# The shifted bias written and read back in four pieces, and the memory's attention begun beside q's last unit

## The reference, cut to what matters

```
z = h @ w_in                                    # mixer; one of its parts is dilated attention, which
bias = rel_bias_table[bucket].transpose(2,0,1)  # adds a bias for each head and each distance q - k
q = (h @ wq).reshape(b, s, 4, 128)              # memory cross attention: 4 heads of 128
scores = einsum('bshd,bmhd->bhsm', q, k) * 128 ** -0.5
o = einsum('bhsm,bmhd->bshd', softmax(scores), v).reshape(b, s, 512)
return o @ wo
```

## Time and profile before

| | |
|---|---|
| median of 3 runs | 2355.29 us (2349.98 to 2355.97) |
| the profiled execution, its time and its span | 2355.84 us, 2354.1 us |
| TensorE busy | 2253.3 us, 96% of the span |
| VectorE, ScalarE, GpSimd busy | 1362.3, 1067.9, 62.9 us |
| share of TensorE in the chain that ended last | 65% |

### The profile page before, as it was taken

How to read it: one execution, slowest core, us unless ns; L and a number is a source line. 1 busy time by engine, 2 the same in 40 slices (tenths; PEclk the granted TensorE clock), 3 DMA queues, 4 the chain that set the end, 5 groups by cost and what they waited for, 6 DMA issues and landing times.

```text
span 2354.1 us, 31707 instructions
## 1 busy us (share of the span) xinstructions
PE 2253.3 (96%) x12978; PEld 1959.9 (83%) x12978; DVE 1362.3 (58%) x1718; ACT 1067.9 (45%) x1376; POOL 62.9 (3%) x66
## 2 busy tenths in 40 slices
PE   8799999888989999999999999999999999999998
PEld 7788898787877888888888888888986889889776
DVE  5446666566556666767666444655445555544554
ACT  5343542424455544544555334545435443544443
POOL 0000101002000000000000000000000000000000
PEclk9899999899989999999999999999999999999999
DMA  7756440014634555555565555553550556445143
GB/s 279 189 191 202 163 158 1 1 32 154 203 118 134 190 185 188 186 187 187 186 206 191 190 192 196 185 195 120 181 178 19 180 178 222 159 152 174 59 129 140
DMA packets 237804, 375.59 MB, mean 160 GB/s; under 512 B 8535, under 2 KB 110072, under 8 KB 236920
## 3 DMA queue, kind: packets, MB, share of 16 engines
q1 hardware_dynamic: 229596, 362.83, 46.3%
q10 hardware_dynamic: 8092, 11.11, 1.9%
HBM read 369.45 MB, written 4.46 MB: 159 GB/s over the span
## 4 chain that ended last, share of the span: by engine, by line
PE 65%; issue 5%; DVE 4%; ACT 2%; POOL 0%; DVEq 0%; POOLq 0%; ACTq 0%
PE PS L482 16%; PE PS L441 12%; PE PS L443 12%; PE PS L442 12%; PE PS L485 8%; DVE w_lo L359 1%; PE PS L2062 1%; ACT w_hi L354 1%; PE PS L2152 1%; PE PS L2136 1%; PE PS L2046 1%; PE PS L2827 1%; DVE h_both L938 0%; PE PS L921 0%; ACT spare L2074 0%
## 5 line engine op out<-in xcount | busy, mean ns | idle before, releaser
L359 DVE TENSOR_TENSOR w_lo<-raw,w_hi 128x2048 fp32r<-128x2048 f32 (+2 forms) x340 | 766.8, 2256 | 765.2 <-ACT w_hi L354 765.0
L354 ACT ACTIVATE w_hi<-raw 128x2048 fp32r<-128x2048 f32 (+2 forms) x340 | 641.2, 1886 | 876.0 <-PE PS L443 494.4
L482 PE MATMUL PS<-h_both,w_hi 128*128 128x512 f32 x1968 | 541.6, 397 | 12.2 <-DVE w_lo L359 9.4
L441 PE MATMUL PS<-w_hi,h_both 128*128 128x512 f32 (+2 forms) x1344 | 514.9, 383 | 11.7 <-DVE h_both L943 4.5
L442 PE MATMUL PS<-w_lo,h_both 128*128 128x512 f32 (+2 forms) x1344 | 507.2, 377 | 0.0
L443 PE MATMUL PS<-w_hi,h_both 128*128 128x512 f32 (+2 forms) x1088 | 408.3, 375 | 0.0
L482 PEld LDWEIGHTS PS<-h_both,w_hi 128*128 128x128 f32 x1968 | 338.1, 190 | 59.4 <-ACT arena L609 9.6
L485 PEld LDWEIGHTS PS<-h_both,w_lo 128*128 128x128 f32 x1968 | 303.2, 189 | 42.2
L485 PE MATMUL PS<-h_both,w_lo 128*128 128x256 f32 x1968 | 314.0, 281 | 0.0
L441 PEld LDWEIGHTS PS<-w_hi,h_both 128*128 128x128 f32 x1344 | 254.3, 189 | 60.0 <-issue 6.0
L442 PEld LDWEIGHTS PS<-w_lo,h_both 128*128 128x128 f32 x1344 | 254.6, 189 | 45.4
(11 more groups left out here) (569 smaller groups left out, 2003.4 us busy)
## 6 DMA issues: line engine op xcount, KB each, us to landing
raw<-in_w_in SPq DMA_DIRECT2D x132, 1024.0 KB, 5.0
raw<-in_ffn_w_up SPq DMA_DIRECT2D x176, 512.0 KB, 4.3
raw<-in_w_out SPq DMA_DIRECT2D x48, 1024.0 KB, 5.1
raw<-in_ffn_w_down SPq DMA_DIRECT2D x44, 1024.0 KB, 5.0
raw<-in_mem_wkv SPq DMA_DIRECT2D x8, 1024.0 KB, 11.5
raw<-in_mem_wq SPq DMA_DIRECT2D x4, 1024.0 KB, 5.1
raw<-in_mem_wo SPq DMA_DIRECT2D x4, 1024.0 KB, 7.2
raw<-in_w_in SPq DMA_DIRECT2D x4, 768.0 KB, 4.6
```

The costliest lines, as they stand in the source:

```text
L354: act.activation(w_hi[:, slot % 2, :st.n], raw[:, slot, :st.n], ACT.Copy).then_inc(hi_made, 1)
L359: dve.tensor_tensor(w_lo[:, slot % 2, :st.n], raw[:, slot, :st.n], w_hi[:, slot % 2, :st.n].bitcast(F32), ALU.subtract).then_inc(lo_made, 1)
L441: pe.matmul(ps, l_hi, r_hi, start=start, stop=False, skip_group_check=skip)
L482: pe.matmul(sums, wh[:, k, cs], h_both[:, :, kk, :], start=kk == 0, stop=False, skip_group_check=True)
```

## The change

**The bias** is written in four pieces of three heads, each by a DMA of its own, and read back in four pieces. ScalarE issues the writes in stage C, after it has rounded C0, C2, C4 and C6; after C10 it waits for all four writes, issues the first read, and issues the others after C11, C12 and C13. The waits for `rel_back` ask for 64.

**The memory.** Units 2 and 3 of MEM_Q are laid by heads: each holds the rows 1024 to 2047, unit 2 for the columns of heads 0 and 1, unit 3 for those of heads 2 and 3. The attention of heads 0 and 1 begins in the middle of unit 3, that of heads 2 and 3 behind it. Stage MEM_O begins with the blocks of heads 0 and 1 for g0, then turns the rest, then takes the first half of g1, then the second halves of g0 and g1.

```diff
-        ST_MEM_Q = Stage(count, "mem_q", w_cols(I["mem_wq"][0], 0), 1, ch=(0, 512))
+        def mem_q_unit(g, j):
+            return mem_q_rows[:, 4 * j:4 * j + 4, :] if j < 2 else mem_q_rows[:, 8:16, (j - 2) * S:(j - 1) * S]
+        ST_MEM_Q = Stage(count, "mem_q", mem_q_unit, 1, ch=(0, 512))
...
+        def multiply_heads(pe, q, j, ready=None):
+            bank, slot = 2 * q.parity + j - 2, (q.first + j) % 2
...
+            for n, (c, k) in enumerate(order):
+                if n == 8:
+                    if ready:
+                        ready()
+                    yield
...
+        def beside_mem_tensor(pe):
+            yield from multiply_heads(pe, Group(ST_MEM_Q, 0), 3)
+            yield from rounds(4)
+            lanes_made(pe, mem_lanes[:2])
+            turn_pair_tensor(pe, t_o, 0, blocks_of(o_mem))
+            yield
+            pe.wait_ge(t_o.dve, t_o["lo0"])
+            multiply_blocks(pe, Group(ST_MEM_O, 0), 0)
+            lanes_made(pe, mem_lanes[2:])
+            turn_pair_tensor(pe, t_o, 1, blocks_of(o_mem))
+            multiply_blocks(pe, Group(ST_MEM_O, 1), 0)
+            pe.wait_ge(t_o.dve, t_o["lo1"])
+            for g in range(2):
+                multiply_blocks(pe, Group(ST_MEM_O, g), 2)
+            for g in range(2, 4):
+                multiply(pe, Group(ST_MEM_O, g), 0)
+            yield
...
+        def bias_scalar(act):
+            for n in range(4):
+                hs = slice(3 * n, 3 * n + 3)
+                act.dma_start(shifted[hs], arena[hs, WROW:WROW + 384].unsqueeze(1).to_broadcast([3, P, 384]))\
+                   .then_inc(rel_out, 16)
+                yield
+                yield
+            yield
+            yield
+            act.wait_ge(rel_out, 64)
+            for n in range(4):
+                act.dma_start(rel_bias[:, 3 * n:3 * n + 3, :],
+                              bass.AP(shifted.tensor, 3 * n * 384 * P + P - 1, [[383, P], [384 * P, 3], [1, S]]))\
+                   .then_inc(rel_back, 16)
+                yield
...
-            act.dma_start(shifted, arena[0:A_H, WROW:WROW + 384].unsqueeze(1).to_broadcast([A_H, P, 384])).then_inc(rel_out, 16)
...
-            act.wait_ge(rel_out, 16)
-            act.dma_start(rel_bias, bass.AP(shifted.tensor, P - 1, [[383, P], [384 * P, A_H], [1, S]])).then_inc(rel_back, 16)
-            run(products_scalar(act, ST_C, before=end_of(ST_BC), more=True))
+            weave(products_scalar(act, ST_C, before=end_of(ST_BC), more=True), bias_scalar(act))
```

More of the change, by code:

```diff
@@ L335, in load_units @@
                     sp.wait_ge(lo_made, q.unit(j - 3))
-                dst, src = raw[:, slot, :st.n].rearrange("p (k n) -> p k n", k=st.kb), st.src(q.g, j)
+                kb = 8 if st is ST_MEM_Q and j >= 2 else st.kb
+                dst, src = raw[:, slot, :st.n].rearrange("p (k n) -> p k n", k=kb), st.src(q.g, j)
                 if isinstance(src, tuple):
@@ L496, in multiply, with multiply_blocks @@
             last.then_inc(unit_used, 1)
+        def multiply_heads(pe, q, j, ready=None):
+            bank, slot = 2 * q.parity + j - 2, (q.first + j) % 2
+            pe.wait_ge(lo_made, q.unit(j + 1))
+            wh = w_hi[:, slot, :].rearrange("p (k n) -> p k n", k=8)
+            wl = w_lo[:, slot, :].rearrange("p (k n) -> p k n", k=8)
+            order = [(c, k) for kh in range(2) for c in range(2) for k in range(4 * kh, 4 * kh + 4)] if j == 2 else \
+                    [(c, k) for c in range(2) for k in range(8)]
+            for n, (c, k) in enumerate(order):
[3 more added lines that the diff above has]
+                    yield
+                cs = slice(c * P, (c + 1) * P)
+                last = three_pass(pe, PS[:, bank, c * S:(c + 1) * S], wh[:, k, cs], wl[:, k, cs], h_hi[:, 8 + k, :],
+                                  h_lo[:, 8 + k, :], False, k == 7, True)
+            last.then_inc(unit_used, 1)
+            yield
+        def multiply_blocks(pe, q, k0):
+            st, bank, slot = q.st, (2 * q.parity, 2 * q.parity + 1), q.first % 2
+            if k0 == 0:
+                pe.wait_ge(act_evac, q.number(-1))
+                pe.wait_ge(dve_evac, q.number(-1))
+                pe.wait_ge(lo_made, q.unit(1))
+            wh = w_hi[:, slot, :].rearrange("p (k n) -> p k n", k=4)
+            wl = w_lo[:, slot, :].rearrange("p (k n) -> p k n", k=4)
+            for t in range(TB):
+                for k in (k0, k0 + 1):
+                    ts = slice(t * P, (t + 1) * P)
+                    last = three_pass(pe, PS[:, bank[t], :], h_hi[:, k, ts], h_lo[:, k, ts], wh[:, k, :], wl[:, k, :], k == 0,
+                                      k == 3)
+            if k0:
+                last.then_inc(unit_used, 1)
         def products_tensor(pe, st, opening=None, row=None):
@@ L1844, in dilated_vector @@
             if h < 2:
[L1845 removed]
+                dve.wait_ge(rel_back, 64)
             for t_, (o, n) in enumerate(DILATED):
@@ L2232, in mem_starts, with late_mem_starts @@
             pe.wait_ge(act_evac, ST_MEM_Q.G1)
+        def late_mem_starts(pe):
             pe.wait_ge(dve_evac, ST_MEM_Q.G1)
@@ L2236, in hybrid_two_blocks, with mem_attention, beside_mem_scalar, beside_mem_vector @@
                           lambda h: v_mem[:, :, h * P:(h + 1) * P], put_mem, plain_put)
-        mem_lanes = on_lanes(mem_heads, lanes_of(len(lanes), [5] * M_H), mem_starts)
+        mem_rooms = [dict(lanes[n], bank=4 + n, s=ar(at, 512), p=ar(at + 512, 512))
+                     for n, at in enumerate((8704, 9728, 10752, 18176))]
+        mem_lanes = on_lanes(mem_heads, [[0], [1]], mem_starts, mem_rooms[:2]) + \
+            on_lanes(mem_heads, [[2], [3]], late_mem_starts, mem_rooms[2:])
+        def mem_attention(e, part, beside):
+            run(together(*[after(1, lane_jobs(part, e, m)) for m in mem_lanes[:2]],
+                         *[after(2, lane_jobs(part, e, m)) for m in mem_lanes[2:]], beside))
+        def beside_mem_tensor(pe):
[15 more added lines that the diff above has]
+            yield
+        def beside_mem_scalar(act):
+            yield
+            yield
+            yield
+            split_hi(act, Group(ST_MEM_O, 1), 0)
+            yield from rounds(4)
+            turn_pair_scalar(act, t_o, 0)
+            yield
+            turn_pair_scalar(act, t_o, 1)
+            yield
+        def beside_mem_vector(dve):
+            yield
+            yield
+            evac_vector(dve, end_of(ST_MEM_Q))
+            yield
+            split_lo(dve, Group(ST_MEM_O, 1), 0)
+            yield from rounds(4)
+            turn_pair_vector(dve, t_o, 0)
+            yield
+            turn_pair_vector(dve, t_o, 1)
+            yield
         act_ff = ar(0, FB * S)
@@ L3233, in _ @@
             run(products_tensor(pe, ST_OUT, out_opening_tensor(pe)))
[L3234 to L3240, removed]
+            block, ready = blocks_of(x), quarters_ready(add_out)
+            for n in range(4):
+                turn_pair_tensor(pe, t_memq, n, block, ready)
+            for u in range(2):
+                pe.wait_ge(t_memq.dve, t_memq[f"lo{4 * u + 3}"])
+                multiply(pe, Group(ST_MEM_Q, 0), u)
+                for n in (4 + 2 * u, 5 + 2 * u):
+                    turn_pair_tensor(pe, t_memq, n, block, ready)
+            pe.wait_ge(t_memq.dve, t_memq["lo11"])
+            run(multiply_heads(pe, Group(ST_MEM_Q, 0), 2, lambda: pe.wait_ge(t_memq.dve, t_memq["lo15"])))
+            mem_attention(pe, lane_tensor, beside_mem_tensor(pe))
             up_tensor(pe, opening_tensor(pe, ST_UP, t_ffn, blocks_of(x), quarters_ready(add_mem)), n_ffn)
@@ L3299, in _ @@
             run(products_scalar(act, ST_OUT, opening=out_opening_scalar(act), ahead=ST_MEM_Q))
[L3300 to L3303, removed]
+            run(unscaled_opening_scalar(act, ST_MEM_Q, t_memq, gain_of("g_mem"), squares_scalar(act, n_memq)))
+            q = end_of(ST_MEM_Q)
+            act.wait_ge(unit_used, q.unit(3))
+            ST_MEM_Q.scalar_evac(act, q)
             split_hi(act, Group(ST_MEM_O, 0), 0)
-            for n in range(2):
-                turn_pair_scalar(act, t_o, n)
-            run(products_scalar(act, ST_MEM_O, made=1, ahead=ST_UP))
+            mem_attention(act, lane_scalar, beside_mem_scalar(act))
+            for g in range(1, 4):
+                run(group_scalar(act, Group(ST_MEM_O, g), Group(ST_MEM_O, g - 1), int(g == 1)))
+            split_hi(act, Group(ST_UP, 0), 0)
+            last_scalar(act, end_of(ST_MEM_O))
             up_scalar_program(act, unscaled_opening_scalar(act, ST_UP, t_ffn, gain_of("g_ffn"), squares_scalar(act, n_ffn)))
@@ L3387, in _ @@
             some(quarters, 2)
-            run(products_vector(dve, ST_MEM_Q, more=True,
-                                opening=unscaled_opening_vector(dve, ST_MEM_Q, t_memq, gain_of("g_mem"), quarters)))
+            run(unscaled_opening_vector(dve, ST_MEM_Q, t_memq, gain_of("g_mem"), quarters))
             mem_scale_vector(dve)
```

(10 more changed lines are left out.)

8 lines of the change are left out of this document (7 added, 1 removed).

## The result

The changed kernel took 2358.05 us (median of 20 runs, 2350.38 to 2361.74), the kernel before 2354.24 (20 runs, 2349.90 to 2355.97): a ratio of 1.0017, 95% interval 1.001 to 1.0024. That is some 4 us slower and the same within 0.3%, where 30.5 us slower, 2386, was forecast. The profiled execution of after took 2350.9 us, near the lowest of its runs, and that of before 2355.84, near the highest. So the two spans are not set against each other; places in them are.

What follows compares the result with a forecast made beforehand. TensorE, busy 96% of the span, was taken to bound the kernel. To 2355.8 us came +30.5 for the bias (C11 27.6 later plus 2.9 of lower clock) and 0 for the memory: 2386, range 2342 to 2412.

Steps and rivals of the forecast that it cites:

- the forecast's own case: Stage C: ScalarE's wait for the writes behind C10 sets the end; own range 2368 to 2405, chance 0.45.
- the case that got least: Stage C: something between, the wait behind C10 passed with 0 to 15 us of loss; chance 0.05.
- Removed, 12.3 us: TensorE's stop ahead of C0 goes: 9.40 us of wait and 2.87 of lower clock.
- the 70 us of exclusive time of three engines: Bias write: all four pieces go over the same three engines and take 70 us, between bounds 32 and 116.
- The sum around it: Packets start at 91.3, plus 70 of write and 28.6 of loads: wait ends at 190, C11 starts 27.6 us later.
- Late loads: Stage C: loads beside the write take 10 us and more to landing; counted inside the same sum, nothing added.
- The rival in which they set the end: Stage C: late loads, not the wait, starve TensorE from C5 on; 2378 to 2400 us, chance 0.2.
- The rival on the other side: Bias: the pieces cost nothing, if pieces and loads together take less than 60 us; 2343 to 2345, chance 0.17.
- The limit of each engine, 116 us: Bias write: each engine's own 0.226 us a packet holds, 116 in place of 70; +46, 2432 us, chance 0.13.
- The memory, 0 between -2.7 and 2.8: Memory's attention and MEM_O: g0 3.1 us earlier, g2 idle 3.7; 2.7 gained or 2.8 lost to lower clock, taken as 0.
- The share below 19%: Sign of being right: the write's share near 3 / 16 (19%) of the engines; above 19% would show it wrong.
- the loads above 10 us: Sign of being right: loads in stage C take 10 us and more to landing.

Runs made afterwards that it cites:

- spread rows: The kernel before with four bias pieces behind C0, C2, C4 and C6, wait behind C10, and table rows on every fourth partition: ratio 0.9949.
- the pieces further apart: The kernel before with the bias part alone, but pieces behind C0, C3, C6 and C9 and the wait behind C15: ratio 0.9962.
- the run with the early wait and no holds: The kernel before with the bias part alone, but pieces behind C0, C3, C6 and C9, wait still behind C10: ratio 1.004.
- the run with the late wait: The kernel before with the bias part alone, pieces behind C0, C2, C4 and C6, but the wait behind C15: ratio 1.0001.
- one write over twelve engines: The kernel before with one write of all twelve rows behind C0, no pieces, the wait and one read behind C10: ratio 0.9972.
- the part alone: The kernel before with only the memory part of the change: ratio 1.0007.
- the best kernel: The kernel before with its one write from rows on every fourth partition, and the memory part with g0 finished before g1: 2336.62 us, ratio 0.9942.
- g0 finished first: The kernel before with the memory part alone, but g0 of the last stage finished before g1 is begun: ratio 0.9984.

## Why the prediction was wrong, step by step

The time lies inside the range 2342 to 2412 and on the slower side, but outside the 2368 to 2405 of the forecast's own case. It is nearest to the case that got least, 0.05: the wait behind C10 passed with 0 to 15 us of loss. C11 started at 169.74, 14.3 us behind the 155.4 of no wait; with 2.6 of lower clock and without the 12.3 removed that is the 4.6 of the bias.

- **Removed, 12.3 us: right.** C0 on TensorE at 92.56 without a wait, and C0 to C3 at 5.61 us (92.56, 98.17). The rounding of C2 is 13.5 us earlier than before (98.43 against 111.90). The runs that pay little for the write keep 12.4 to 13.4 us of it at CE0's place.
- **The failed step: the 70 us of exclusive time of three engines.** From the packets' start to the end of the wait the write's share was 10.7% of 16 engines (90 to 165 us, 1548 packets), 128 us of engine time, **43 us** for each of three. The trace splits it: 14.7% until 106 us, 0.141 us a packet, then:

```profile
q10 hardware_dynamic: 1281, 1.95, 9.7%
```

  from 106 to 165 us, 0.097 x 16 x 59 / 1281 = 0.071 us a packet. The reasoning that the three rows of a piece are neighbours and share a limit was right for the start (17.4% for 65 packets from 94 to 98 us: 0.17 us each) and spread rows show it as such. What I took for the whole was true for the first 15 us.

  Why it went away is shown in part. The second piece doesn't end it: with the pieces further apart that piece is issued only at 105.07, and a packet takes 0.144 us from 104 to 106 and 0.069 from 106 to 108 all the same (14.4% for 32, 7.6% for 35), as the queue's mean falls from 2.3 engines at a time to 1.2. And the limit comes back at the end of the run with the early wait and no holds, where no load lies beside and the last piece's rows are left, 160 to 168 us:

```profile
q10 hardware_dynamic: 134, 0.21, 12.3%
```

  That is 2.0 engines, 0.118 us a packet, 26 GB/s; three engines at 0.17 us made 25 from 94 to 98. So what is limited is the group of neighbouring rows, at some 25 GB/s, whether three engines read from it or two. Loads that keep an engine busy, and engines that are no longer abreast (two of three are left here), would take the readers of one group apart; that is argued, as the trace doesn't name engines.
- **The sum around it: right.** With 43 in place of 70, 91.3 + 43 + 28.6 = 163 against 164.96 measured. C11 then follows by the same chain, 4.8 us behind (5.3 forecast), 2.0 late, and 2.6 of lower clock (2.9 forecast): +4.6 for +30.5. The forecast's mechanism held, the wait behind C10 set the end; the term was off by 27. The pieces from spread rows bear the sum out: 10.1% of 16 engines from 90 to 151.7 us are 33 us for each of three, and 91.3 + 33 + 28.6 = 153 against 151.7. That both come within 2 us is luck in part. A load's packet took 0.095 us in after (47.4% for 5983 packets from 90 to 165 us) where rows 8 gave 0.081, and with it the sum for after would be 168.
- **What wasn't in the sum at all: the held issues.** I costed an issue at 0.4 us on ScalarE's idle time. Two of them cost 12 us by themselves, as the run with the late wait shows. In the change they don't show in the time, since any delay ahead of the wait is taken out of the wait: it lasted 10.39 us, not some 40. Had I mended the term alone I would have come near the time and missed a cost of 12 us that the wait hides.
- **Late loads: right that they come, right not to add them.** 9 to 19 us to landing, and no stop of TensorE is theirs in after. The rival in which they set the end is refuted at this delay; at 20 to 26 us, with one write over twelve engines, they do stop it once.
- **The rival on the other side** decided at 60 us for pieces and loads together. They took 73.7 (91.2 to 164.9), so it stayed just out of reach. **The limit of each engine, 116 us:** refuted by the packets at 0.071 and 0.065.
- **The memory, 0 between -2.7 and 2.8: right in kind, one bound just passed.** g0 in its stage 3.3 us earlier (698.72 less the 0.9 of this trace against 701.04), g2's idle 3.71 for 3.7, its clock low behind it (0.60 from 714 to 717 us); -1.4 us in after, +3.2 in the part alone, which is 0.4 beyond the bound. The sum feared the lower clock for g0 and g2. In the part alone it came behind the 1.63 us ahead of the product with v (2.9 us) and behind g2's stop, in after only behind the latter, so which of the two values came out was chance.
- **The share below 19% and the loads above 10 us** came as written and told nothing apart, since both hold for 43 us too. The issue of the first read, at 164.96, was the observation that did.
- **The 18 us** named as cover between the fourth issue and C11 were wrong: from 122 to C11's rounding, due at 149 (87.8 + 11 x 5.61), are 27. Nothing in the sum rests on it.

## What to carry to other kernels

A wait that is due at a fixed time is a bound by itself: what delays the engine ahead of it costs nothing until the wait is moved, and what looks like the culprit in the trace may be hidden behind it; undo one at a time. Before a transfer is cut in pieces, ask which partitions it reads: the same write from every fourth partition took away the whole stop, with no piece and no wait moved. When an engine that computes issues a large DMA behind another, count what is still to move; the issue itself may be what it waits for.

## What the runs showed of the hardware

**An issue can hold its engine's queue until enough has moved.** At the end of each held issue the packets still to move were, by the queue's counts (387 to a piece, the issue's own included), 1161 - 597 = 564 and 1548 - 977 = 571, a mean of 188 and 190 for each of three engines. Issues that weren't held ended at 608 (after, second), 561 and 587 (pieces further apart), 633 (spread rows, third), and the spread rows' fourth, held 3.72 us, at 635. It isn't the sum that counts: the one write behind C0 was issued in 1.42 us with all its 1548 packets still to move, 129 for each of twelve engines. With three engines an issue is held near 190 to 210 for each. Held and unheld ones overlap there; engines that drift apart would explain it, as these are means, and that is argued.

**The lower clock behind a stop isn't a fixed price.** The same stop of 3.7 us was followed by 3.4 and by 6.1 us of products at 0.43 us. The same stop of 1.63 us, ahead of the product with v, cost nothing in after and in the best kernel (3.84 us), 1.6 us with g0 finished first (5.47) and 2.9 us in the memory part alone (6.77). The stop of 2.15 us in after had no lower clock behind it (1.00 from 141.5 to 146 us), nor had those of 1.41 and 0.99 us in the memory's part.
